# Two-layer decoder trunk: raw residual into the products with 1/rms applied at PSUM, token block 0 first at the layer borders, and a reordered second mixer

## What is computed

```python
def rms_norm(x, g):
    y = xf * lax.rsqrt(jnp.mean(xf * xf, axis=-1, keepdims=True) + NORM_EPS)
    return (y * g.astype(jnp.float32)).astype(x.dtype)
...
h = rms_norm(x, norm_mix[layer])
...
p = h @ w_in_ab[i]
...
x = x + jnp.concatenate([a_out, b_out], axis=-1) @ w_out_ab[i]
x = x + swiglu(rms_norm(x, norm_ffn[layer]), ffn_w_gate[i], ffn_w_up[i], ffn_w_down[i])
...
def short_conv_mixer(bg, cg, xz, w):
    z = cg * xz
...
    y = sum(w[t] * zp[:, t:t + s] for t in range(CONV_TAPS))
    return bg * y
```

## Time and profile before

| | |
|---|---|
| three runs | 1452.85, 1454.38, 1455.74 us; median 1454.38 |
| profiled execution | 1455.55 us in all, of which the span is 1453.8 us (1.75 us lie around it) |
| PE busy | 1417.9 us, 98% of the span |
| DVE, ACT, POOL busy | 81%, 70%, 4% |
| experts | from 469.3 us of the span to its end |

### The profile page before, as it was taken

How to read it: one execution, slowest core, us unless ns; L and a number is a source line. 1 busy time by engine, 2 the same in 40 slices (tenths; PEclk the granted TensorE clock), 3 DMA queues, 4 the chain that set the end, 5 groups by cost and what they waited for, 6 DMA issues and landing times.

```text
span 1453.8 us, 20345 instructions
## 1 busy us (share of the span) xinstructions
PE 1417.9 (98%) x7058; PEld 1177.7 (81%) x7058; DVE 1184.7 (81%) x1457; ACT 1021.4 (70%) x1229; POOL 55.8 (4%) x75
## 2 busy tenths in 40 slices
PE   7998999989999999999999999999999999999998
PEld 5787999978888788888888888888888888888886
DVE  5865555556645999999999999999999999999998
ACT  4655444454655777877877887787787788778776
POOL 0010000000230000000000000000000000000000
PEclk9999999999999999999999999999999999999999
DMA  9940643541039999999999999999999999999980
GB/s 353 319 169 26 230 180 116 183 151 72 1 136 396 350 359 372 349 386 358 350 390 372 363 363 368 373 355 389 370 334 389 373 367 360 378 369 346 385 311 29
DMA packets 183568, 430.28 MB, mean 296 GB/s; under 512 B 5385, under 2 KB 13109, under 8 KB 183520
## 3 DMA queue, kind: packets, MB, share of 16 engines
q1 hardware_dynamic: 180528, 421.24, 78.3%
q0 software_dynamic: 2304, 5.78, 2.1%
q10 hardware_dynamic: 688, 2.62, 0.4%
HBM read 425.09 MB, written 7.34 MB: 297 GB/s over the span
## 4 chain that ended last, share of the span: by engine, by line
PE 93%; DVE 4%; ACT 2%; issue 1%; DMA 0%; ACTq 0%; DVEq 0%
PE psum L672 29%; PE psum L673 29%; PE psum L674 29%; PE psum L1144 2%; DVE w_lo L370 1%; PE psum L861 1%; PE psum L699 1%; PE psum L770 1%; PE psum L794 1%; PE psum L887 1%; PE psum L1125 0%; ACT w_hi L362 0%; DMA x_residual<-in_x 0%; DVE x_residual L1854 0%; PE psum L780 0%
## 5 line engine op out<-in xcount | busy, mean ns | idle before, releaser
L388 DVE TENSOR_TENSOR w_lo<-raw_ring,w_hi 128x1024 fp32r<-128x1024 f32 x674 | 814.0, 1223 | 70.7 <-ACT w_hi L383 57.5
L383 ACT ACTIVATE w_hi<-raw_ring 128x1024 fp32r<-128x1024 f32 x675 | 714.6, 1062 | 193.2 <-PE psum L674 190.1
L672 PE MATMUL psum<-w_hi,xg_hi 128*128 128x512 f32 x896 | 357.9, 399 | 1.7 <-DVE xg_lo L1998 0.9
L674 PE MATMUL psum<-w_hi,xg_lo 128*128 128x512 f32 x896 | 353.7, 395 | 0.0
L673 PE MATMUL psum<-w_lo,xg_hi 128*128 128x512 f32 x896 | 353.6, 395 | 0.0
L370 DVE TENSOR_TENSOR w_lo<-raw_ring,w_hi 128x1024 fp32r<-128x1024 f32 x124 | 151.8, 1227 | 134.6 <-ACT w_hi L362 133.9
L362 ACT ACTIVATE w_hi<-raw_ring 128x1024 fp32r<-128x1024 f32 x124 | 130.1, 1056 | 130.1 <-PE psum L674 127.5
L674 PEld LDWEIGHTS psum<-w_hi,xg_lo 128*128 128x128 f32 x896 | 168.0, 187 | 40.9
L672 PEld LDWEIGHTS psum<-w_hi,xg_hi 128*128 128x128 f32 x896 | 168.0, 188 | 40.8 <-issue 2.1
L673 PEld LDWEIGHTS psum<-w_lo,xg_hi 128*128 128x128 f32 x896 | 168.2, 188 | 38.7
L672 PE MATMUL psum<-w_hi,moe_hT_hi 128*128 128x512 f32 x448 | 178.4, 398 | 0.0
(11 more groups left out here) (249 smaller groups left out, 1289.3 us busy)
## 6 DMA issues: line engine op xcount, KB each, us to landing
raw_ring<-in_moe_w_gate SPq DMA_DIRECT2D x56, 2048.0 KB, 10.1
raw_ring<-in_moe_w_up SPq DMA_DIRECT2D x56, 2048.0 KB, 10.2
raw_ring<-in_moe_w_down SPq DMA_DIRECT2D x56, 2048.0 KB, 9.8
raw_ring<-in_ffn_w_gate SPq DMA_DIRECT2D x5, 2048.0 KB, 9.8
raw_ring<-in_ffn_w_up SPq DMA_DIRECT2D x5, 2048.0 KB, 8.0
raw_ring<-in_ffn_w_down SPq DMA_DIRECT2D x5, 2048.0 KB, 9.1
raw_ring<-in_w_in_ab SPq DMA_DIRECT2D x4, 2048.0 KB, 19.8
raw_ring<-in_w_in_cd SPq DMA_DIRECT2D x4, 2048.0 KB, 9.4
```

The costliest lines, as they stand in the source:

```text
L383: act.activation(wh[:, v % SPLITS, :], moe_raw(i, q), ACT.Copy).then_inc(hi_ready, 1)
L388: dve.tensor_tensor(wl[:, v % SPLITS, :], moe_raw(i, q), wh[:, v % SPLITS, :].bitcast(F32), ALU.subtract).then_inc(lo_ready, 1)
L672: pe.matmul(out_, sh, mh_, start=start, stop=False)
L674: return pe.matmul(out_, sl, mh_, start=False, stop=stop)
```

## The change

1. **No norm ahead of the products.** `x_T` transposes the raw residual, `x_hi` and `x_lo` multiply by the gain alone. Each of these works on half of one token block, 512 columns: four instructions of 128 columns each. The squares, the root and the reciprocal run later, beside the products. 1/rms is applied where a result leaves PSUM: as the scale of ACT's copies when tokens are partitions, which makes `evict` two instructions of 512 columns in place of one of 1024; and where tokens are columns (SwiGLU from slab 1, convolution) by a row of 1/rms on all partitions. That row comes from a diagonal (DVE), one matmul with ones (`spread_scale`, PE) and a copy (`copy_scale`, ACT), once for n = 1 and once for n = 2.
2. **Block 0 first.** `first_tile` runs the first four units for block 0, then for block 1, with block 1's transposes between. `residual` is split by blocks; ahead of n = 1 and n = 2 the last output or down units run for block 0 first, and block 0's transposes are put between their block-1 parts.
3. **SwiGLU.** Slab 0 is computed like a projection (tokens as partitions) and its product then transposed (`h0_T`, 8 transposes). For the other 18 blocks DVE first scales the gate out of PSUM, ACT's Silu reads that, then DVE multiplies as before.
4. **Loads.** Block 0 of x, the mixer gains and the identity come first, tile 0 in four quarters, then block 1 of x; the other constants and parameters go behind tile 1.
5. **First mixer.** `heads_T` is cut at 3, not at 4.
6. **Second mixer.** All of k's RoPE is on DVE, in four parts, with two low parts of weights behind part 0 and one each behind parts 2 and 3. The last projection tile moves ahead of the k transposes and scores, on ACT with it the two next high parts and the copy of v (two instructions). The convolution's copies move to DVE with the scale (`conv_scaled`). `C_FILL` has no half at items 7 and 8 and one at 9; the first `c_cat_T` stands ahead of the last `c_turn`.

```diff
@@ loads (SP)
-            sp.dma_start(xres[:, :, :], x[0].rearrange("(t p) d -> p t d", p=P)).then_inc(x_loaded, 16)
-            sp.dma_start(cst[:, :], const_f32).then_inc(const_loaded, 16)
+            sp.dma_start(xres[:, 0, :], x[0, 0:P, :]).then_inc(x_loaded[0], 16)
+            sp.dma_start(par_rows[R_MIX:R_MIX + 16, :], norm_mix.rearrange("l (k p) -> (l k) p", p=P)).then_inc(mix_loaded, 16)
+            sp.dma_start(cst[:, C_ID:C_ID + P], const_f32[:, C_ID:C_ID + P]).then_inc(ident_loaded, 16)
...
+                    for q in range(4):
+                        sp.dma_start(dst[:, 2 * q:2 * q + 2, :], src[:, 2 * q:2 * q + 2, :]).then_inc(
+                            quarter_loaded[q] if q < 3 else slot_loaded[0], 16)
+                    sp.dma_start(xres[:, 1, :], x[0, P:2 * P, :]).then_inc(x_loaded[1], 16)
@@ PE
+            def x_T(n, t, half):
...
+                for kk in range(4):
+                    k = 4 * half + kk
+                    mm = pe.transpose(ps[:, xT_banks[n][t] + half, kk * P:(kk + 1) * P],
+                                      xres[:, t, k * P:(k + 1) * P], ident)
+                mm.then_inc(xt_done, 1)
+            def first_tile(n, u0, later_rows):
+                for tt in range(TT):
+                    sl = slice(tt * P, tt * P + P)
+                    for i in range(4):
...
+                        pe.wait_ge(xt_lo, 8 * n + 4 * tt + i + 1)
...
+                        if tt == 0 and i == later_rows:
+                            x_T(n, 1, 0)
+                            x_T(n, 1, 1)
+            def spread_scale(n):
+                pe.wait_ge(diag_ready, n)
+                pe.matmul(ps[:, 6, 0:SEQ], cst[:, C_ONE:C_ONE + P], row_scale[:, 1, :], start=True, stop=True).then_inc(
+                    row_scale_done, 1)
...
-                for tt in range(TT):
-                    for n in (2, 3):
-                        ab_unit(n, (tt,))
+                ab_unit(2, (0,))
+                ab_unit(3, (0,))
+                ab_unit(2, (1,))
+                x_T(1, 0, 0)
+                ab_unit(3, (1,))
+                x_T(1, 0, 1)
...
                 c_heads_q()
+                project(U_V4, first["conv"], 1, 4)
                 c_heads_k(0)
                 c_score(0)
                 c_score(1)
-                project(U_V4, first["conv"], 1, 4)
                 c_heads_k(1)
...
-                    c_turn(n)
                     if n == C_N - 1:
                         c_cat_T(0)
+                    c_turn(n)
...
+                mm.then_inc(sum_done, 1)
+                for i in range(4):
+                    down(nblk - 4 + i, u + i, (1,)).then_inc(unit_used, 1)
+                    if i < 2:
+                        x_T(2, 0, i)
...
-            heads_T(0, 4)
+            heads_T(0, 3)
             project(U_V4L, first["out_ab"], 0, 5)
-            heads_T(4, 6)
+            heads_T(3, 6)
@@ ACT
+            def begin_ffn():
+                split_hi(act, U_FFN)
+                split_hi(act, U_FFN + 1)
+                act.wait_ge(col_ready, 2)
+                x_hi(1, 0, 0)
+                split_hi(act, U_FFN + 2)
+                x_hi(1, 0, 1)
+                split_hi(act, U_FFN + 3)
+                x_hi(1, 1, 0)
+                x_hi(1, 1, 1)
+                act.preload_act_table(ACT.Sqrt)
+                row_square(1, 0)
...
-                act.activation(dst, ps[:, b:b + TT, 0:ncol], ACT.Copy).then_inc(proj_act, 1)
+                for tt in range(TT):
+                    ins = act.activation(dst[:, tt, :], ps[:, b + tt, 0:ncol], ACT.Copy, scale=small[:, RS + tt:RS + tt + 1])
...
                 c_heads_q()
+                split_hi(act, U_V4 + SPLITS)
+                split_hi(act, U_V4 + 1 + SPLITS)
+                act.wait_ge(unit_used, first["conv"])
...
                 c_heads_k(0)
                 c_exp(0)
-                split_hi(act, U_V4 + SPLITS)
                 c_exp(1)
...
+                            act.wait_ge(gate_scaled, j + 1)
+                            act.activation(fsg[:, j % 2, :], fsg[:, j % 2, :], ACT.Silu).then_inc(fsg_ready, 1)
@@ DVE
+            def begin_ffn():
+                split_lo(dve, U_FFN)
+                split_lo(dve, U_FFN + 1)
+                residual(0, 0)
+                x_lo(1, 0, 0)
+                split_lo(dve, U_FFN + 2)
+                x_lo(1, 0, 1)
+                residual(0, 1)
+                split_lo(dve, U_FFN + 3)
+                x_lo(1, 1, 0)
+                x_lo(1, 1, 1)
...
+                dve.tensor_tensor(row_scale[:, 1, :], row_scale[:, 0, :], row_scale[:, 0, :], ALU.mult).then_inc(row_square_ready, 1)
...
+                for w in range(4):
+                    t, h0 = divmod(w, 2)
+                    c_rope_part(dve, link, c_rope, 1, t, 6 * h0, 6, (None, k0_roped, None, k1_roped)[w])
...
+                for w in range(2):
+                    split_lo(dve, U_V4 + w + SPLITS)
                 c_max(0)
                 c_max(1)
-                for w in range(2):
-                    split_lo(dve, U_V4 + w + SPLITS)
...
+                            dve.wait_ge(unit_used, u + 1)
+                            dve.tensor_tensor(fsg[:, j % 2, :], ps[:, b % 2, 0:SEQ], row_scale[:, 0, :], ALU.mult).then_inc(gate_scaled, 1)
```

More of the change, by code:

```diff
@@ L1443, in ffn @@
             def ffn():
-                u = first["ffn"]
-                for s in range(len(widths) + 1):
+                act.wait_ge(rstd_ready, 2)
+                act.wait_ge(unit_used, U_FFN + 4)
+                for t in range(TT):
+                    act.activation(fh0[:, t, :], bank(t), ACT.Silu, scale=small[:, RS + t:RS + t + 1]).then_inc(silu0_ready, 1)
+                for u in range(U_FFN + 8, U_FFN + 12):
+                    split_hi(act, u)
+                copy_scale(1)
+                u = U_FFN + 8
+                for s in range(1, len(widths) + 1):
                     if s < len(widths):
@@ L1470, in _ @@
             attention()
[L1471 to L1474 removed]
+            begin_ffn()
             ffn()
[L1477 to L1478 removed]
+            begin_cd()
+            project_cd(U_IN, U_V4)
             c_attention()
@@ L1882, in _ @@
+            begin_x()
             project_ab()
```

532 lines of the change are left out of this document (326 added, 206 removed).

## The result

Four executions of the changed kernel in the first job took 1432.75 to 1433.44 us, median **1432.87 us**, against a median of 1455.01 us before: ratio 0.9852, 95% interval 0.9836 to 0.9867, so 1.5% less. The forecast was 1433.2 (range 1428 to 1440). The kernel before has two groups as well, 1452.85 to 1454.38 and 1455.29 to 1455.93 us (and one execution of 1470.83), so a median depends on how many of each it holds. The span went from 1453.8 to 1431.1 us.

The account below looks back on a forecast made before the run. PE, busy 1417.9 of 1453.8 us, was taken to bound the kernel, so only less work, waiting or low clock helps. Terms summed to -21.2 us: profiled 1455.55 becomes 1434.4, median 1433.2, range 1428 to 1440.

Parts of the forecast that it names:

- (b): Rival: no fall of the clock in the second mixer, 2.1 and up to 1 us less, 1430.3; chance 0.2.
- Start: Kernel start: first product at 9.7 us, tile 0 done at 23.6; -2.4 us, range -1.0 to -3.5.
- First mixer: Last tile covers k's RoPE with the cut at 3, -1.85 us; evict of two instructions, +0.1.
- Borders and SwiGLU: Border 1 -7.4 us, border 2 -7.85; eight added SwiGLU transposes +1.0, two rows of 1/rms +0.5 each.
- rival (e): Borders do less, as narrow instructions cost like wide ones: 2.2 us more in each of three places, 1439.8; chance 0.08.
- Second mixer's entry: Waits of 2.0 and 2.7 us replace the old ones; -1.8 us, with a low-clock stretch +0.3 in all.
- so I expect one again: 6.8 us at 0.50 ... 2.1 us: Second mixer's entry: a low-clock stretch of 6.8 us, 2.7 of it on the wait, costing 2.1 us.
- Second mixer's end: Turns 8 and 9 covered, output units at 427.4: -4.05 us; about 0 if cover fails and the clock falls.
- GpSimd's RoPE moved to DVE: Second mixer's entry: GpSimd's share of the RoPE goes to DVE as a fourth part of 2.3 us.
- Rival (c): Clock falls at both waits of the second mixer's entry, each with transposes beside it: 2.1 us more, 1435.3; chance 0.08.
- rival (f): Slower: in 18 SwiGLU blocks the hop DVE, ACT, DVE sets the pace, say 1476 us; chance 0.04.

Follow-up runs that it names:

- the short-entry run: Changed kernel with ScalarE copying k earlier and DVE taking two maxima ahead of two low parts at the second mixer's entry; median 1428.89 us, ratio 0.9825.
- the small products: Unused products on zeros added at the start: 15 and 12 on the changed kernel, 1433.86 us; 8 and 8 with ScalarE and DVE reordered at second mixer's entry, 1428.24.
- the run with the scaling four times: Changed kernel with DVE doing the gate's scaling four times in a row instead of once in 18 SwiGLU blocks; median 1433.43 us.
- the second execution: Profiled execution of the changed kernel run once more, unchanged; that run's median 1435.44 us.

## Why the prediction was right, and where it was not

**Right, as a sum**: -21.2 us forecast, -22.6 between marks, -22.1 as medians. Two terms were wrong by 1.3 and 2.1 us, with opposite signs; the borders gave 1.0 more and the first mixer and the second one's end 0.2 less each. That the profiled execution lies within 1.5 us of the forecast (1432.88 for 1434.4) is in part luck, and so is the 0.3 us at the median, as the forecast took it from 1454.38 and the median before was 1455.01 in the end. The lower bound of 1428 is also lower than its own reason: (b), 1430.3, with the start's best, 1.1 more, is 1429.2.

**Start, -2.4 forecast, -1.14 measured: mis-sized.** The loads, the halves (1.13 to 1.16 us for a group of four, 1.1 forecast) and the first product (9.97 for 9.7) came as said. "I let the clock rise near 13.3" did not: it rose at 15.5, and S stood 15.07 us behind the first product where 13.9 was forecast. In the short-entry run it rose at 13.4 and S stood 14.04 us behind. The eleven traces without the small products lie between these two in order: 14.04 us with the rise 3.25 us behind the first product, 14.48 with 4.23, 15.02 with 5.44, 15.07 with 5.53. So the time of the rise is the size that was wrong; behind the first product PE waits for no low part in either of the two traces. The Trainium skill ("TensorE: Matmul & The Clock Gate", Part 1) says that the gate's timing is not tied to the kernel's start, so the point of the rise varies from run to run; the traces agree, with rises between 13.4 and 15.6 us for first products between 9.6 and 10.3.

**First mixer, -1.75 forecast, -1.57 measured**; putting the cut back cost 1.82. Right; the scores came 2.7 us earlier in all (81.84 for 84.55), not 4, for want of the start's part.

**Borders and SwiGLU, -13.25 forecast together** (-7.4 + 1.0 + 0.5 - 7.85 + 0.5), -14.21 measured (the marks cut them otherwise). Of the 1.0 more, 0.5 is the two rows that spread 1/rms, 0.24 us each for the 0.5 that I took from the row; how the rest divides was not followed further than this: the transposes were priced too high as well, the eight of slab 0 cost 0.79 us for 1.0, the sixteen of border 2 1.5 for 2.0. That is 1.2 in all, so some 0.2 us went elsewhere. The low price of the narrow instructions, on which rival (e) hung, was right: four take 1.12 us.

**Second mixer's entry, +0.3 forecast, -1.85 measured: the step that failed**, and the largest miss of the sum, is "so I expect one again: 6.8 us at 0.50 ... 2.1 us". Its two waits and its 17.5 us from q's turning to the first turned item (17.46) were right to 0.1 us. No low stretch came in the first trace, which is rival (b). But (b) is right for that execution only. Over the eight traces that share this entry, the clock fell ahead of the first turned item in four, just behind it in two, and near it in neither way in two. Ahead of it a fall of 3.4 us cost nothing (three traces), as the wait behind it shrank from 2.79 to 1.24 us, and one of 6.8 us, which left no wait at all, cost at most 0.65 (the run with the scaling four times: 17.57 and 61.78 for 17.46 and 61.24); behind it 3.4 us cost 1.5. I had taken one cost for a thing whose place isn't fixed.

**Second mixer's end, -4.05 forecast, -3.82 measured**: right in its steps. From the lists, turn 9 came 1.44 us nearer to the first turned item (33.63 us for 35.07), as forecast; from turn 9 to the first output unit it took 3.84 us, forecast 3.55, for 4.88 before; from there to the router 23.77 for 25.12, the 1.35 us of cold products of the forecast. What the sum doesn't tell is how much of this hangs on the clock. By the old end put back, the order alone gives 0.7 us, and 3.15 is the low clock that follows the 1.79 us wait in the old order. The forecast named that as its condition ("if the clock falls, about 0") and the second execution shows it in part: with a fall of half the length, 1.5 us of it were gone.

**GpSimd's RoPE moved to DVE, forecast inside the entry.** GpSimd had one of k's four parts (6 of 24 heads, a quarter and not a sixth). The old order in the new kernel takes 20.32 us against 19.31 before, which fits 1 us for the fourth part on DVE; this is argued from two kernels that differ in more than that.

**SwiGLU, rival (f)**: DVE 20.66 of 36 us, forecast under 26; excluded with a margin of over 1.26 us a block. Rival (c), the clock falling at both waits of the entry, was seen in no trace. No run was made on whether transposes keep the clock up; the reading of the earlier trace rows stands as it was.

## What to carry to other kernels

Sum the waits, but ask of each stall what clock comes behind it and what work will run there: the same fall cost nothing where another engine's chain set the next start and PE had a wait to lose, and half its length where products followed. When an order is changed to remove a wait on one engine, walk the queues of the other engines at that place too: here the whole entry gained 1.85 us over the kernel before, and putting copies and maxima ahead of splits on ScalarE and DVE another 3.2. A filler that is meant to hold the clock must be measured at the low clock, and only helps if what comes after it is set by TensorE.

## What the runs showed of the hardware

- One program on one core gives two groups of times 2 us apart. Two traces, one of each group, differ by where the granted clock falls behind waits of 0.87 to 2.8 us; the same wait is followed by a fall in one execution and not in the next.
- A wait of 3.38 us for DVE's residual had 0.50 behind it in the one trace that has it, and in one of 4.04 us the clock fell 1.1 us before its end; behind the waits of 0.2 us at that border no other trace has a fall.
- A fall of 3.4 us costs 1.5 us on products and 0.0 where a wait of 2.79 us for another engine stands behind it, which then shrinks to 1.24; one of 6.8 us cost 3.15 on products.
- Small products of 128 columns on zeros, whose result nobody uses, raised the clock: it rose at 4.9 and 5.4 us, where it rose at 13.4 to 15.6 without them. They took 0.47 us each at first, 0.24 after (3.78 and 1.95 us for eight).
- Stretches with the same instructions repeat to 0.05 us over 13 traces; all that varies is the start (1.2 us from the earliest to the latest S without warming) and where the clock is low.
